# One Trainium2 core, two transformer layers: first expert entered chunk by chunk, output computed ahead of the overflow look, one more weight slab split early

## What is computed

```python
for layer in range(2):
    mod = silu(c) @ w_mod[layer] + b_mod[layer]        # six vectors of 1024: shift, scale, gate, twice
    h = rms_norm(x, g1) * (1 + scale1) + shift1
    p = h @ w_in[layer]                                # q, k, v, neighbourhood q, k, v, pooling, gates
    x = x + gate1 * (merge(attention(p), pool(p)) @ w_out[layer])
    h = rms_norm(x, g2) * (1 + scale2) + shift2
    if layer == 0:
        x = x + gate2 * swiglu(h, w1, w3, w2)          # hidden width 2816
    else:                                              # 8 experts, hidden width 3584, top 2 per token
        logits = h @ router_w + router_b
        combine = softmax over the two largest, zero elsewhere
        x = x + gate2 * sum(combine[:, e] * swiglu(h, w1[e], w3[e], w2[e]) for e in range(8))
out = rms_norm(x, final_g)
```

## Time and profile of the kernel before

| | |
|---|---|
| median of three runs | 2302.3 us (2302.21 to 2302.62) |
| the profiled execution's own time | 2298.58 us |
| its span | 2296.8 us |
| PE busy | 2139.9 us, 93% of the span |
| POOL, DVE, ACT busy | 1281.2, 1149.8, 1049.0 us |
| mean granted clock of PE | 0.961 of full speed |
| chain that ended last | PE 45%, POOL 36%, issue 13%, DVE 3%, DMA 2%, ACT 1% |

### The profile page before, as it was taken

One profiled execution on the slowest core, in us unless ns is written; L12 is line 12 of the kernel. 1 busy time (PEld: TensorE's weight loads), 2 busy tenths in 40 slices (PEclk: granted clock), 3 DMA queues, 4 the chain that ended last, 5 costly groups with the idle time before them and its releaser, 6 DMA issues.

```text
span 2296.8 us, 27513 instructions
## 1 busy us (share of the span) xinstructions
PE 2139.9 (93%) x10742; PEld 1589.5 (69%) x10743; DVE 1149.8 (50%) x1362; ACT 1049.0 (46%) x1134; POOL 1281.2 (56%) x464
## 2 busy tenths in 40 slices
PE   5987899999999996887997999999999999999996
PEld 4874676647787875765985677676767777776774
DVE  2146211131010103255324888878778787878775
ACT  4224321024222124123313666766666666667664
POOL 3300233015445454200411989888988989988994
PEclk7999999999999998899997999999999999999998
DMA  7226521221223222224435999999999999989992
GB/s 308 94 93 234 202 80 73 92 108 58 92 95 107 88 78 73 84 99 186 161 135 237 348 348 345 357 341 346 344 341 345 348 339 354 357 334 353 339 351 99
DMA packets 69641, 503.17 MB, mean 219 GB/s; under 512 B 7744, under 2 KB 7872, under 8 KB 9088
## 3 DMA queue, kind: packets, MB, share of 16 engines
q1 hardware_dynamic: 68976, 497.92, 58.1%
q0 software_dynamic: 528, 3.41, 0.4%
HBM read 500.24 MB, written 1.05 MB: 218 GB/s over the span
## 4 chain that ended last, share of the span: by engine, by line
PE 45%; POOL 36%; issue 13%; DVE 3%; DMA 2%; ACT 1%; SPq 0%; POOLq 0%; ACTq 0%; DVEq 0%
POOL moe_lo L476 35%; PE bank L726 10%; PE bank L727 10%; PE bank L728 10%; PE bank L741 7%; PE bank L754 2%; DMA slab<-in_w_in 2%; PE turned L929 2%; PE pv_bank L948 1%; PE bank L908 1%; DVE s_mx L1806 1%; POOL w_lo L440 1%; DMA moe_slab<-in_moe_up 0%; DVE PT L1829 0%; ACT H_NEW L1326 0%
## 5 line engine op out<-in xcount | busy, mean ns | idle before, releaser
L476 POOL TENSOR_TENSOR moe_lo<-moe_slab,moe_hi 128x512 fp32r<-128x512 f32 x336 | 922.0, 2768 | 178.6 <-ACT moe_hi L1515 177.1
L476 DVE TENSOR_TENSOR moe_lo<-moe_slab,moe_hi 128x1536 fp32r<-128x1536 f32 x336 | 691.8, 2064 | 178.8 <-ACT moe_hi L1515 176.3
L440 POOL TENSOR_TENSOR w_lo<-slab,w_hi 128x2048 fp32r<-128x2048 f32 (+2 forms) x72 | 297.9, 4138 | 736.7 <-ACT w_hi L1285 736.6
L1515 ACT ACTIVATE moe_hi<-moe_slab 128x2048 fp32r<-128x2048 f32 x336 | 629.1, 1905 | 0.0
L726 PE MATMUL bank<-moe_hi,HE_HI 128*96 128x512 f32 x896 | 361.6, 404 | 8.9 <-issue 5.3
L726 PE MATMUL bank<-H_HI,w_hi 128*128 128x512 f32 (+1 forms) x880 | 325.2, 370 | 34.2 <-POOL w_lo L440 24.7
L728 PE MATMUL bank<-moe_hi,HE_LO 128*96 128x512 f32 x896 | 354.7, 396 | 0.0
L727 PE MATMUL bank<-moe_lo,HE_HI 128*96 128x512 f32 x896 | 352.9, 394 | 0.0
L727 PE MATMUL bank<-H_LO,w_hi 128*128 128x512 f32 (+1 forms) x880 | 321.4, 365 | 0.0
L728 PE MATMUL bank<-H_HI,w_lo 128*128 128x512 f32 (+1 forms) x880 | 320.9, 365 | 0.0
L1285 ACT ACTIVATE w_hi<-slab 128x2048 fp32r<-128x2048 f32 (+1 forms) x72 | 135.6, 1883 | 179.2 <-PE bank L728 162.7
(11 more groups left out here) (193 smaller groups left out, 2465.4 us busy)
## 6 DMA issues: line engine op xcount, KB each, us to landing
moe_slab<-in_moe_up SPq DMA_DIRECT2D x224, 1024.0 KB, 4.8
moe_slab<-in_moe_w SPq DMA_DIRECT2D x112, 1024.0 KB, 4.8
slab<-in_w_mod SPq DMA_DIRECT2D x40, 1024.0 KB, 4.8
slab<-in_w_in SPq DMA_DIRECT2D x38, 1024.0 KB, 4.8
slab<-in_ffn_w SPq DMA_DIRECT2D x30, 1024.0 KB, 4.7
start_slab<-in_w_mod SPq DMA_DIRECT2D x8, 1024.0 KB, 17.6
slab<-in_w_proj SPq DMA_DIRECT2D x8, 1024.0 KB, 6.9
slab<-in_w_out SPq DMA_DIRECT2D x8, 1024.0 KB, 4.8
```

What stands on the lines that cost most here:

```text
L440: engine.tensor_tensor(lo, raw, hi.bitcast(F32), ALU.subtract).then_inc(done, 1)
L476: engine.tensor_tensor(moe_lo[n][:, blocks, :], moe_slab[k % MOE_RING][:, blocks, :], moe_hi[n][:, blocks, :].bitcast(F32), ALU.subtract). ...
L1515: af(moe_hi[k % MOE_SPLIT][:], moe_slab[k % MOE_RING][:], ACT.Copy).then_inc(moe_hi_ready, 1)
```

## The change

1. `mod(22)` and `mod(23)` leave the second norm of layer 1 and are made in layer 1's attention: `mod(17)` ahead of the scores in pair 1, `mod(20)` ahead of those in pair 3, all others one behind each pair. The turns move with them.
2. Slab 1 of layer 1's w_in is rounded by ACT right behind the norm's root; its low part is shared, 1536 columns on DVE ahead of chunk 2, 512 on POOL ahead of the H_LO chunks.
3. The router's products and the turns to token layout go chunk by chunk of H; the two logits have a bank each, one turn goes to the bank `turned[1]`. ACT copies half of HTOK. The position and ONEHOT come before the weights. PE gathers once ONEHOT is there, and waits for the copies of HTOK that each half reads.
4. Expert slabs 0 and 1 are rounded and split during layer 1's output product, 2 and 3 are rounded around the exponential. SP loads 0 to 3 behind the last gate, 4 to 6 behind the last product of w_out; the ring's places are turned by three.
5. The last down slab is rounded and split one place earlier. The last expert's quarters go to four banks and PE waits for none of the additions.
6. The output is computed ahead of the overflow look: squares per quarter added (ACT), a sum over chunks and partitions by PE with a matrix of ones, a root and a reciprocal over 128x256, six chunks of the output on DVE, two scaled on ACT and multiplied on POOL, DMAs in the order 0, 6, 2, 4. The register load comes before the output on SP and POOL, behind it on PE and ACT, and in step 6 of the stream on DVE. If the branch is taken, all is computed again.

The diff, cut to its core:

```diff
-MOD_IN_ATTENTION = (range(4, 16), range(16, 22))
-MOD_IN_NORM = (22, 23)
+MOD_IN_ATTENTION = (
+    [((p + 2) // 2 if p and p % 2 == 0 else None, None, 4 + p) for p in range(12)],
+    [(None, None, 16), (None, 17, 18), (8, None, 19), (9, 20, 21), (10, None, 22), (None, None, 23)])
+LAST_TURNED = (7, 11)
...
-SHARED = [("in", 0, 0), ("in", 0, 1)] + [("in", 1, s) for s in range(2, 19)]
+SHARED = [("in", 0, 0), ("in", 0, 1)] + [("in", 1, s) for s in range(1, 19)]
...
-        moe_slab = [at(f"moe_slab{i}", 8 * i, [P, 4, 512]) for i in range(MOE_RING)]
+        moe_slab = [at(f"moe_slab{i}", 8 * ((i + RING) % MOE_RING), [P, 4, 512]) for i in range(MOE_RING)]
...
-            if key == ("in", 0, 1):
+            if key[0] == "in" and key[2] == 1:
                 return 3 * SLAB // 4
...
+            wait_full(sp, ("gate", 1, 3, 2, 1))
+            for k in range(MOE_RING - RING):
+                stream_load(k)
             wait_full(sp, ("out", 1, 3, 1))
-            for k in range(RING, MOE_RING):
-                stream_load(k)
-            wait_full(sp, ("mod", MOD_PAIRS - 1))
-            for k in range(RING):
+            for k in range(MOE_RING - RING, MOE_RING):
                 stream_load(k)
...
@@ POOL
-            next_low_part()
+            for _ in range(2):
+                next_low_part()
             h_low_parts((1, 1))
@@ PE route
+                for k in range(DC):
+                    pe.wait_ge(h_ready[1, 2], k + 1)
+                    for t in range(2):
+                        ins = mm(logits[t][:, 0:N_EXPERTS], H[:, k, S + P * t:S + P * t + P],
                                  VEC[:, lo:lo + N_EXPERTS], start=k == 0, stop=k == DC - 1)
+                    half, c = divmod(k, 4)
+                    for t in range(2):
+                        ins = nc.tensor.transpose(tokens[2 * half + t][:, P * c:P * c + P], ...)
...
@@ ACT squares ahead of the second norm
                 squares((layer, 2), lo, hi, range(0, 4), out_added)
+                else: stream_high(0)
                 squares((layer, 2), lo, hi, range(4, 6), out_added)
+                else: stream_high(1)
@@ DVE residuals of layer 1
+                    if norm_key == (1, 2) and c in (4, 6):
+                        stream_low_part(dve, v, c // 2 - 2, slice(0, LO_DVE), moe_lo_dve)
@@ DVE norm
+                    if key == (1, 1) and c == 2:
+                        low_half(1)
@@ ACT and DVE stream
                     if n + 1 < STEPS:
                         high(("up", n + 1, 0))
+                    else:
+                        high(("down", n))
...
+            def final(again):                                   # ACT
+                for c in range(DC):
+                    act.wait_ge(x_added, ... 4 * (N_EXPERTS - 1) + c // 2 + 1)
+                    af(SQF[:, c, :], XT[:, c, S:T], ACT.Square).then_inc(sqf_ready, 1)
+                for c in LAST_CHUNKS:
+                    af(OUT[:, c, :], XT[:, c, S:T], ACT.Copy, scale=VEC[:, lo + c:lo + c + 1])
+                act.wait_ge(stat_ready, again + 1)
+                af(RMSF[:], up[0][:, 0:S], ACT.Sqrt, scale=1.0 / D, bias=eps).then_inc(final_rms, 1)
+            def final(again):                                   # DVE
+                v.reciprocal(RINVF[:], RMSF[:]).then_inc(final_rrms, 1)
+                for c in range(LAST_CHUNKS[0]):
+                    v.scalar_tensor_tensor(OUT[:, c, :], XT[:, c, S:T], VEC[:, lo + c:lo + c + 1], RINVF[:],
+                                           ALU.mult, ALU.mult).then_inc(out_ready, 1)
+            def final(again):                                   # POOL
+                for c in LAST_CHUNKS:
+                    nc.gpsimd.tensor_tensor(OUT[:, c, :], OUT[:, c, :], RINVF[:], ALU.mult).then_inc(out_pool, 1)
```

More of the change, by code:

```diff
@@ L161, in schedule @@
         for p in range(len(pairs)):
-            if p and p % 2 == 0:
-                turned_mod(MOD_IN_ATTENTION[layer][p - 1] // 2)
+            group, before, behind = MOD_IN_ATTENTION[layer][p]
+            if group is not None:
+                turned_mod(group)
+            if before is not None:
+                mod(before)
             scores(p + 1, 0)
             scores(p + 1, 1)
-            mod(MOD_IN_ATTENTION[layer][p])
-        turned_mod(MOD_IN_ATTENTION[layer][-1] // 2)
+            mod(behind)
+        turned_mod(LAST_TURNED[layer])
         fills.extend(("pool", layer, p) for p in range(2))
@@ L1241, in _ @@
             route()
-            for i in range(4):
+            for i in range(3):
                 wait_taken(pe, ("turn", i))
-            pe.wait_ge(counts_ready, 2)
-            gather(0)
+            wait_taken(pe, ("prefix",))
+            gather(0, (htok_act, htok_dve))
             stream()
@@ L1839, in attention @@
                     turned_out(2 * p)
-                    if p and p % 2 == 0:
-                        turned_mod(mods[p - 1] // 2)
+                    group, before, behind = MOD_IN_ATTENTION[layer][p]
+                    if group is not None:
+                        turned_mod(group)
+                    if before is not None:
+                        mod(before)
                     if p + 1 < pairs:
                         maxima(2 * p + 2)
-                    mod(mods[p])
+                    mod(behind)
                     turned_out(2 * p + 1)
```

280 lines of the change are left out of this document (154 added, 126 removed).

## The result

The changed kernel takes 2269.64 us (median of 4 runs, 2266.96 to 2270.95); the kernel before, run beside it, took 2302.26. The ratio is 0.9867, with a 95% interval of 0.985 to 0.9885: by the ratio 30.6 us less, between 26 and 35 (the two medians differ by 32.6). The forecast was 2264.0. The profiled execution took 2268.39 us with a span of 2266.5, against 2298.58 and 2296.8 before: 30.3 us less in the span.

The account below looks back on a forecast made before the run. PE was taken as the bound, busy in every microsecond of the expert stream, with removable gaps elsewhere. Terms -15.8 + 5.4 - 19.5 - 8.4 = -38.3 us took the median 2302.3 to 2264.0 us, range 2254 to 2274.

Parts of the forecast that it names:

- Entry: Start of layer 1: splitting slab 1 before the chunks lets PE start at about 907.6; -15.8 us, bounds 7.8 to 16.8 gained.
- the first 17 took 0.222 us each, 3.8 us slow: Entry of layer 1: 3.8 us of products at the lower clock, then 79 at 0.121 us, chain's end at 921.
- The rival of a clock that stays low to the chain's end: Chance 0.12: PE waits between chunks, works at 0.222 us instead of 0.121; entry of layer 1 gains only 7.8; time 2272.
- Attention: Layer 1's attention: two pairs with a second modulation product, each 2.7 us late; +5.4 us, bounds nothing to 13.7.
- The product takes 1.93: Attention: after the second slab of mod(17) lands at 1019.5, its product takes 1.93 us, ending at 1021.4.
- Router and expert: Second norm to first expert product: 15.7 us earlier, plus 3.8 from stall and lower clock behind it; -19.5 us, bounds 15.2 to 22.2.
- I take 1223.6, near the rows' rate: Router: time of the last logits, between 1220.9 (PE as fast as H comes) and 1224.1 (1.0 us a chunk).
- The end: Last restart gains 1.5 us, last addition to span's end 6.9; -8.4 us in all, bounds 6 to 11.
- 10.5 and 11.6: Last addition to span's end: 10.5 us by the last DMA's landing, 11.6 by SP's branch; 11.0 taken.
- The look's load in the stream: Expert stream: the overflow look's load on DVE, 0.83 us once, costs nothing; bounds 0 and 4.3.
- the stream that takes the gain back: Rival, chance 0.06: the expert stream only waits later, the router's 19.5 us shrink to nothing; -19, time 2283.
- POOL that slows down: Rival, chance 0.04: POOL becomes the stream's bound; 0.2 us more on each of 336 low parts adds 67; time 2331.

## Why the prediction was right, and where its sizes were off

PE's gap was shorter at each place that was named, and the time lay 5.6 us above the forecast, within its range. In the spans, 38.3 us were forecast and 30.3 came; the eight lines of the table say where the 8.0 went. Two of the reasons given did not hold: the router by chunks of H has no gain that shows, and the price of the moved columns came near the forecast by luck.

**Entry, 1.35 us too much.** The step "the first 17 took 0.222 us each, 3.8 us slow" carried over the old duration of the slow stretch. It now lasted 27 products, 5.9 us: ten more at some 0.1 us, which is 1.0 of the 1.35. The rest lies behind the chain: its end came 14.8 us earlier, the first scores 14.45. The products kept at work in the norm show that this is the clock after idle time, and that 1.2 to 1.6 us lie in it (the broadcast was as slow in the kernel before). The rival of a clock that stays low to the chain's end did not come true. DVE's 1536 columns did stand in the way of H_LO 0, which took 1.48 us where one alone took 1.27: 0.2 us, less than the 0.4 charged. The Trainium skill (SBUF — State Buffer, "Who interferes with whom") has the later of two such instructions blocked. The trace agrees: DVE's ended at 908.53, 1.27 us behind it is 909.80, and H_LO 0 ended at 909.68.

**Attention, 2.0 us too little by the table, 5 like with like.** The waits were there, 3.80 and 3.14 us, the length of a load. "The product takes 1.93" failed: 3.64 and 3.11, behind an idle PE. Counted from the first scores by the columns that both kernels have, the two pairs with a second column grew by 3.7 and 2.8 us, 6.5 for the 5.4 forecast. The pairs behind each of them grew by 1.6 and 1.1, for which the forecast had nothing. And the first pair, which the change leaves as it was, is 1.6 us shorter. That last figure is luck. In six profiles with this order of PE in attention the first column stands 7.7 us behind the first scores and attention takes 87.5 to 88.8 us; in four others it stands 9.1 to 9.3 us behind and attention takes 90.5 to 91.0. The kernel before is of the second kind (9.34), so its attention is to be compared with the 90.55 us of the run with the columns alone, which has the same 9.34: the two columns cost 10.5 us, twice the forecast.

**Router and expert, 0.9 us too much in all** (12.44 for 15.7, and 7.63 less the last restart's 1.4, so 6.2, for 3.8). "I take 1223.6, near the rows' rate": that is 10.7 us behind the norm's sums, and the last logits stood 13.0 us behind them. The chunks took 1.17 us, not 1.0, all at the granted clock 0.50, which is 1.2 of the 2.3. DVE's part to SEL was 0.3 shorter than counted. The gather was put behind ONEHOT alone, but it waits also for DVE's copies of the turned banks: 0.8 us, as the run without that wait shows. DVE's addition to POS took 0.86 us beside a low part of POOL, where such small ones take 0.17: 0.7. That makes the gather 3.5 us late, and the way from there to the first expert product came as counted (5.65 us, forecast 5.9). The forecast credits the earlier gather to the chunks of H; the run with the columns alone has it at 18.9 us with the old router, so it is the norm without the columns that brought it, and the chunks added nothing that shows. Against this, the first steps gave more than was counted: the run without early splits lost 6 us behind its first expert product, where the forecast had 2.3 of stall and 1.5 of clock. The term at nothing was the slow start of the stream itself, at the clock 0.50 behind PE's wait of 5.34 us.

**The end, 1.7 us too much.** The branch of "10.5 and 11.6" that is nearer is the upper one: SP's jump does stand at the end, though what comes next without it is only 0.4 to 0.9 us shorter. "Two squares 0.9" and "PE's last sum 0.7" together measured 2.55 (the last addition ends at 2253.84, the sums at 2256.38), since the 16 products take 0.43 us a chunk and had just begun when the last x came. From the last output to the last issue it took 0.8 us, counted at 0.3. Reciprocal 1.75 (1.8), six outputs 3.49 (3.7), last restart 1.4 (1.5): these held. The look's load in the stream showed no cost.

**The rivals** of the stream that takes the gain back and of POOL that slows down are out: PE's 50.00 of 50 us and POOL's 2750 ns are those of before.

What stays open: why attention has two lengths with one order of work. They part in the first pair, where the granted clock is 1.00 from 990 to 1000 us in the changed kernel (first scores at 991.1) and 0.69 from 990 to 995 in the run without a look (first scores at 986.0), with the same order of work on PE. What lowers it in one and not in the other no run showed. The timed executions also lie in two groups, for the kernel before as for the changed one (on one chip 2294.0 to 2295.1 and 2300.4 to 2302.5), further apart than the 3 us of attention; a median of four can lie in either.

## What to carry to other kernels

Time removed at a gap of the bounding engine reaches the end if nothing behind has a wait of its own; here 15.5 us did. Work that is taken out of one gap and put beside a ring of buffers pays the load that it serialises: count the distance to the columns on both sides, not to one. And after a gap count the first products at the lower clock for as long as they last, not for as long as they lasted before; work for its own sake held the clock where it fitted into the gap (the entry), and cost time where it did not (attention). Last, when several parts of a change shorten one stretch, run each part alone: here a move that was meant to make room, and is worth nothing by itself, did what was credited to another part.

## What the hardware showed beyond that

- A wide reciprocal on VectorE costs by the column: 1.75 us for 256 columns, against 0.30 for 24.
- PE worked on the router's products without a pause from 1212.1 to 1221.8 us, and the granted clock stayed at 0.50 (1.2 GHz) for the whole of it. In that stretch work alone did not bring it back. In the run with the columns alone PE worked as long without a pause, from 1223.6 on, and the clock was at 1.00 from 1233.6 on.
- With one order of work on PE, attention of layer 1 took 87.5 to 88.8 us or 90.5 to 91.0, and the first scores, where the entry was not edited, came between 984.7 and 991.1 us. The traces of two runs can differ by 3 us in a stretch that no edit touched; only an idle time whose cause has changed, or a mark a few us away, tells a term of 1 us.
- The same wait of 2.28 us ahead of PE's last products was followed by the granted clock 1.00 in the kernel before and by 0.50 in the run with the last slab back at its place.
